# Filler products of a scan on TensorE: pieces of 512 columns placed whole instead of in two halves

## The reference

```python
def _in_proj(h, w_in, names=None):
    out, off = {}, 0
    for name, width in IN_GROUPS:          # q, k, v, f, cs, co, gate
        if names is None or name in names:
            out[name] = h @ w_in[:, off:off + width]
        off += width
    return out

def step(s, inp):                          # the scan over tokens, 8 heads, 2 directions
    w_t, k_t, v_t, kk_t, b_t = inp[:5]
    sk = jnp.einsum('dbhvk,dbhk->dbhv', s, kk_t)
    s = s * w_t[..., None, :] - sk[..., None] * b_t[..., None, :] + v_t[..., None] * k_t[..., None, :]
    y = jnp.einsum('dbhvk,dbhk->dbhv', s, inp[5]) if len(inp) == 6 else None
    return s, y
```

## Time and profile before

| | us |
|---|---|
| median of 3 runs | 3673.91 |
| lowest, highest | 3664.45, 3676.2 |
| profiled execution | 3661.34 |
| its span in the trace | 3659.4 |

### The profile page before, as it was taken

One profiled execution on the slowest core, in us unless ns is written; L12 is line 12 of the kernel. 1 busy time (PEld: TensorE's weight loads), 2 busy tenths in 40 slices (PEclk: granted clock), 3 DMA queues, 4 the chain that ended last, 5 costly groups with the idle time before them and its releaser, 6 DMA issues. The chain is left out here.

```text
span 3659.4 us, 82761 instructions
## 1 busy us (share of the span) xinstructions
PE 3373.4 (92%) x36725; PEld 2692.7 (74%) x36725; DVE 1584.3 (43%) x2538; ACT 1268.5 (35%) x2184; POOL 1074.0 (29%) x645
## 2 busy tenths in 40 slices
PE   6989999999888999799999899999999898879998
PEld 4668887888655777687878676887778666568887
DVE  3243335442277646612112734445453476372224
ACT  3333233333365422321212143334444365233222
POOL 1111132233011512233333232223333114235453
PEclk9999999999999999899999999999999999999999
DMA  7664332342222333233332145334443313423332
GB/s 264 209 203 113 109 111 87 114 130 83 78 72 76 120 124 125 74 122 116 115 121 93 34 154 177 106 110 126 123 129 90 104 58 121 164 85 104 98 98 87
DMA packets 444861, 423.43 MB, mean 116 GB/s; under 512 B 15652, under 2 KB 372042, under 8 KB 437594
## 3 DMA queue, kind: packets, MB, share of 16 engines
q1 hardware_dynamic: 442922, 409.35, 35.7%
q10 hardware_dynamic: 1584, 8.78, 0.6%
HBM read 329.34 MB, written 88.74 MB: 114 GB/s over the span
## 5 line engine op out<-in xcount | busy, mean ns | idle before, releaser
L888 PE MATMUL ps<-I-322_h_hi,I-325_w_hi 128*128 128x256 f32 (+1 forms) x832 | 297.3, 357 | 4.5 <-PEq L124 4.5
L888 PE MATMUL ps<-I-323_h_lo,I-325_w_hi 128*128 128x256 f32 (+1 forms) x832 | 281.9, 339 | 0.0
L888 PE MATMUL ps<-I-322_h_hi,I-326_w_lo 128*128 128x256 f32 (+1 forms) x832 | 281.4, 338 | 0.0
L2367 POOL TENSOR_TENSOR I-18801_w_lo<-I-18799_w_raw,I-18800_w_hi 128x1024 fp32r<-128x1024 f32 x60 | 144.9, 2415 | 343.5 <-ACT I-18800_w_hi L2330 343.4
L888 PE MATMUL ps<-I-23551_h_hi,I-23554_w_hi 128*128 128x512 f32 (+1 forms) x544 | 211.9, 389 | 4.6 <-PEq L124 4.6
L888 PE MATMUL ps<-I-23552_h_lo,I-23554_w_hi 128*128 128x512 f32 (+1 forms) x544 | 199.9, 368 | 0.0
L888 PE MATMUL ps<-I-23551_h_hi,I-23555_w_lo 128*128 128x512 f32 (+1 forms) x544 | 199.9, 367 | 0.0
L2367 POOL TENSOR_TENSOR I-39041_w_lo<-I-39039_w_raw,I-39040_w_hi 128x1024 fp32r<-128x1024 f32 x60 | 144.4, 2407 | 154.6 <-ACT I-39040_w_hi L2330 154.6
L2330 ACT ACTIVATE I-18800_w_hi<-I-18799_w_raw 128x1024 fp32r<-128x1024 f32 x61 | 64.6, 1060 | 355.6 <-PE ps L365 235.9
L365 PE MATMUL ps<-I-18796_h_hi,I-18800_w_hi 128*128 128x512 f32 x704 | 183.0, 341 | 1.1 <-DVE I-18797_h_lo L402 1.1
L365 PE MATMUL ps<-I-18796_h_hi,I-18801_w_lo 128*128 128x512 f32 x704 | 181.7, 339 | 0.0
(11 more groups left out here) (902 smaller groups left out, 8752.0 us busy)
## 6 DMA issues: line engine op xcount, KB each, us to landing
I-324_w_raw<-in_w_in SPq DMA_DIRECT2D x67, 512.0 KB, 5.9
I-23553_w_raw<-in_w_in SPq DMA_DIRECT2D x67, 512.0 KB, 5.2
I-18809_ada_w<-in_ada_w SPq DMA_DIRECT2D x24, 1024.0 KB, 6.0
I-18799_w_raw<-in_ffn_up SPq DMA_DIRECT2D x44, 512.0 KB, 3.9
I-39039_w_raw<-in_ffn_up SPq DMA_DIRECT2D x44, 512.0 KB, 3.9
proj_d<-I-2000_result SPq DMA_DIRECT2D x52, 384.0 KB, 3.1
I-508_ada_w<-in_ada_w SPq DMA_DIRECT2D x16, 1024.0 KB, 5.6
I-18799_w_raw<-in_ffn_down SPq DMA_DIRECT2D x22, 512.0 KB, 3.4
```

Source lines behind the costliest of these rows:

```text
L888: m = pe.matmul(bank(6 + i % 2, n_c), w[:, k, :], hv[:, k, c0:c0 + n_c], start=k == 0 and v == 0, stop=k == KT - 1 and v == 2)
L2367: pool.tensor_tensor(pair(g)[1], rings[0][:, g % 3, :, :], pair(g)[0].bitcast(F32), ALU.subtract).then_inc(sem("w_lo"), 1)
```

## The change

The halves are gone: each piece is one part, so a piece of 512 columns stands in one place with 24 matmuls. The list ahead of group 0 holds the same pieces as before (five pieces were eight parts), and the three calls of `copy_pieces` there take the same pieces as before.

```diff
@@ -728,13 +728,13 @@
             for i, (s, w) in enumerate(pieces):
-                parts += [(i, s, w, range(0, 4)), (i, s, w, range(4, 8))] if w == BOTH[0] else [(i, s, w, range(8))]
+                parts.append((i, s, w, range(KT)))
...
-            n_first = 8
+            n_first = 5
             share = [(len(parts) - n_first) * (g + 1) // N_G - (len(parts) - n_first) * g // N_G for g in range(N_G)]
@@ -1148,11 +1148,11 @@
-                    copy_pieces(0, "first", some=slice(0, 2))
+                    copy_pieces(0, "first", some=slice(0, 1))
                     decays(0, 0)
-                    copy_pieces(0, "first", some=slice(2, 6))
+                    copy_pieces(0, "first", some=slice(1, 4))
                     decays(0, 1)
-                    copy_pieces(0, "first", some=slice(6, n_first))
+                    copy_pieces(0, "first", some=slice(4, n_first))
```

## The result

The changed kernel takes 3739.12 us (median of four runs, 3735.11 to 3741.69), beside 3672.65 (3664.45 to 3676.2) of the kernel before: a ratio of 1.0187, interval 1.0175 to 1.0200. That is 66 us slower. Forecast were 3724 and a range of 3692 to 3760. The profiled execution took 3740.59 us, 79.3 us more than the one of before (3661.34).

A forecast was written before the change was run, and what follows sets the result against it. TensorE's queue was taken to bound both scans end to end. Saved joins and vanished waits against new waits and lost clock summed to +50 us: 3724 us beside the median of 3673.9, range 3692 to 3760.

The forecast's parts named there:

- Joins saved: Both scans: 98 places without a filler each save 0.31 us of TensorE's queue, -30.4 us.
- price of an emptied place: Both scans: emptied `offT` places cost 0.32 us each, emptied `Y` places 0.6 in the second, together +8.4 us.
- Turn places: First scan: without fillers at `turn0` and `turn1`, TensorE waits for ScalarE's copies at twelve places, +13.8 us.
- Levels 3 and 4: Second scan, groups 0 to 4: TensorE waits while VectorE and ScalarE prepare the next group, +27.4 and +18.3 us.
- `end`: Second scan's group boundaries: five more without a filler wait for the output sum, 1.1 us each, +5.5 us.
- Waits that go: Between first and second S, longer fillers hide L1063's waits for VectorE, with some smaller first-scan ones, -9 us.
- rival 2: Levels 2 to 4 into `W1`: clock stays low, +12 us, and instructions come late, +12; 3748 us, chance 0.12.
- The clock: Second scan, behind the waits of levels 3 and 4: half-clock stretches of 3.4 us, +13.5 us, bounds 0 and 25.
- Rival 1: Levels 3 and 4 of the second scan don't wait, so saved joins decide: faster, 3661 us, chance 0.06.
- Rival 3: `W1` to `S1`, second scan: weight loads and splits fall behind by 1 us a piece, 3760 us, chance 0.05.
- Rival 4: Waits are half of those taken: 3699 us and down to no change, chance 0.13.
- some ten stretches at 0.50: Second scan of the changed kernel: expected sign, about ten stretches with TensorE at half clock.

The follow-up runs named there:

- e7: Whole pieces in the first scan only, placed at both turns and `end` instead of `offT0` to `offT3`; halves in the second scan as in the kernel before: 3673.43 us.
- e1: The changed kernel with whole pieces in the first layer's scan only, halves kept in the second: 3673.84 us, ratio 0.9994 to the kernel before.
- e2: The changed kernel with whole pieces in the second layer's scan only, halves kept in the first: 3741.03 us, ratio 1.0187 to the kernel before.
- e3: The changed kernel with second-layer whole pieces put at levels 3 and 4 first, levels 0 to 2 nearly bare, next inputs issued earlier: 3718.97 us.
- e4b: The changed kernel plus 21 and 13 unread matmuls behind "across" of levels 3 and 4, second scan, groups 0 to 4: 3734.11 us.
- e13: The kernel before, halves kept, with some fillers moved into the middle of each direction's products in both layers: 3701.32 us, ratio 1.0089.
- e4: The changed kernel plus 46 and 30 unread matmuls behind "across" of levels 3 and 4, second scan, groups 0 to 4: 3782.55 us.
- e5: The changed kernel with VectorE's and ScalarE's preparation of the next group moved behind level 4 and the S steps: 3755.4 us.

## Why the prediction was right, and where it was not

- **Joins saved (-30.4)**, with the price of an emptied place (part of the +8.4). The rest of the account holds both: 689.8 to 684.0 in the first scan and 569.7 to 557.6 in the second, -5.8 and -12.1, the same within 1.5 us in every kernel with the same scan. The forecast for the same thing is -30.4 + 8.4 and 3 us of the turns' modelled ends, -19; measured -17.9. Right, though loosely: a part of the +8.4 is idle time ("across" waits 2.6 us for L1300 in the second scan, nothing before).
- **Turn places (+13.8).** L911 and L947 wait 5.6 and 5.1 us behind ScalarE in the first scan, six times each, as forecast; e7 takes them away, and its rest is 4 us lower than e1's. Right.
- **Levels 3 and 4 (+27.4 and +18.3).** The waits came where they were forecast, behind L1286, for the reason forecast, but smaller: +22.9 and +11.3. I take it that TensorE at half clock covers more of VectorE's time with its own blocks (in group 1 "off" of level 3 and "across" of level 4 took 5.05 us, not 2.8); no run shows that share by itself.
- **`end` (+5.5).** +1.8 in the second scan (2.7 against 0.9, three waits and not six, as groups 0 and 1 write no output there); but the first scan got five such waits too, +4.5, which I had left out. **Waits that go (-9):** L1063 -2.7 in the second, 6.7 to 1.4 in the first, together -8.0. Right.
- **Idle time together.** Forecast, without the joins' and modelled shares: 10.8 + 27.4 + 18.3 + 2.7 + 5.5 - 9 = 55.7. Measured 45.4 + 9.6 = 55.0. That it agrees so well is partly luck: 34 for the 46 us of levels 3 and 4, and against it 8.5 us of waits called issue in the second scan (11.8 to 20.3) that I had only in rival 2.
- **The clock (+13.5, bounds 0 and 25).** This is the step that failed: +46.2, outside its bounds. I had priced each wait with the one stretch of 3.4 us that followed the two long waits of the first scan. Behind those waits came S with YR (at 610.24) and a filler (at 869.25). In the second scan of the changed kernel nothing but blocks of the levels follows, and the clock stayed at 0.50 from level 2 or 3 to MV or the end of W1. Rival 2 said so and gave it +12 above the 13.5; it was right in its mechanism, and the excess was 33. With 46 in place of 13.5 the sum is +83, and the two scans are 83 us longer. But the two figures aren't quite the same thing: 13.5 was meant as cost on the path, and 46 counts all time lost at half clock, some of it behind VectorE's work. Read together, levels 3 and 4 with the clock were forecast at 27.4 + 18.3 + 13.5 = 59.2 us and measured at 80.4.
- **The time.** 3739 against 3724, +66 against +50, inside the range, and nearer to rival 2's 3748 than to the forecast. The profiled executions differ by 79, since that of before was 11 us under its median; the account above belongs to that pair. Against that pair, +50 was 29 us short, so that the median came out only 15 us off is in part luck.
- **Rival 1** (joins decide) is out by e2. **Rival 3** (weights late): no wait for POOL of that kind in the changed kernel. **Rival 4** (half the waits) is out: they were three quarters. The mark "some ten stretches at 0.50" was met in number (nine) and wrong in length; "the second scan 45 to 55 us longer" was 79.5.
- **The rule of the Trainium skill** (TensorE: Matmul & The Clock Gate, "HAM oscillation") lays such a loss to the pauses between bursts. The stretch of e3 at 2311 has 0.5 us of pause in 13.4 and stays at 1.2 GHz, so here pauses begin the low stretch and don't explain its length; the measurement decides. The same page's advice to run through the contraction without a break ("Why this matters for your kernels") would have given 3648 by the prediction's estimate; in this kernel the break was what put a filler between the blocks.

**Open.** How much of the 46 us the clock alone costs on the path: at full clock VectorE's waits would be longer (some of the 11.5 us that they fell short). e4b shows it for group 1 alone (4.2 of 6.3 us); in the other groups a low stretch stays or a longer wait called issue comes (up to 3.9 us). And whether e13 would pay with ScalarE's copies placed to match, or why a fetch sometimes comes in time and sometimes not, wasn't tried.

## What to carry to other kernels

In this kernel, filler work between small dependent blocks does three things at once: it covers other engines' turns, it gives the instruction fetches time (in the products, e13), and it brings the matmul clock back. Cutting it in fewer and longer pieces saves 0.1 to 0.25 us a cut here and takes away all three in every place that falls empty, so count the places that need a filler before merging pieces, and keep at least as many pieces. When a wait is priced with its clock, look at what runs behind it: here the low stretch ended in or right behind a filler, or in a later block of the scan, and never while only blocks of the levels ran.

## What the runs showed of the hardware

- **The low clock outlasts its cause.** Within the scans of all 14 traces every low stretch begins at or shortly behind a wait of TensorE of 0.7 us or more, the shorter ones among them in the middle of dense small matmuls; most waits under 2 us have no low stretch behind them (20 of 1 to 2 us in before, none). While only blocks of the levels ran the clock stayed at 0.50, up to 13.4 us with TensorE busy in 12.9 of them (e3, above); it rose while or right after (within 0.8 us) a filler or the added matmuls of e4 and e4b ran or, where none stood, during MV and W1, W2, or S with YR. The two rows below are e5's group 1: levels, then the end of level 4 with MV and W1, after which it was at 1.00.

```profile
2463.50:2476.00 12.50, 10.07 (x299) 9.98 (x301) 2.72 (x10) 1.34 (x6) 0.00 (x0) 0.50 0.02 4
2476.00:2480.60 4.60, 4.60 (x105) 4.60 (x103) 3.98 (x6) 1.18 (x2) 0.00 (x0) 0.50 0.02 5
```

- **A wait called issue goes with an instruction fetch here.** Packets of 16 KB, 1.1 us each, and TensorE goes on 1.1 to 1.7 us behind their end. They stand in runs of some 200 small matmuls at full clock (12 waits in the first scan of before, two in each group's products); in the e3 row, at half clock, 439 small matmuls ran without a wait over 0.3 us. e3 and e4b have 29 and 26 us of such waits over 0.6 us in the second scan, the changed kernel 18.7; since e3's clock loss is as large as the changed kernel's, these runs don't show that a better clock brings them back.
- **A matmul of 128x128 with 128 fp32 columns stands in the trace as two records** 0.111 us apart, 0.223 us together (e4, e4b); one filler matmul with 512 columns costs 0.229. Who plans a block by one record gets one twice as long.
